# The last pack's gate and up weights in k-slices of four experts, and its last down piece as a half and two quarters

## The chip, the cores and the metric

The kernel runs on one core of one Trainium2 chip. The metric is the device time of one execution in microseconds (us); lower is better.

## The reference

The input is 256 tokens of width 1024, f32. A block of two token mixers (a gated short convolution and an S5 state model) is followed by a mixture of experts, and it is this second part that the change touches:

```
h2 = rms_norm(x, norm_ffn)
group, then top 2 of its 8 experts        # 4 groups x 8 = 32 experts
out = 0
for e in range(32):
    a = silu(h2 @ w_gate[e]) * (h2 @ w_up[e])      # 1024 -> 512
    out += combine[:, e] * (a @ w_down[e])         # 512 -> 1024
x = x + out
return rms_norm(x, norm_final)
```

All weights are f32. One expert's gate, up or down matrix is 2 MB, so the 96 of them are about 200 MB, which every execution reads once.

## The kernel before

**Packs.** The 32 experts are taken in 8 packs of 4. Each expert has 32 token slots, so a pack fills 128 slots. TensorE gathers the pack's tokens (L1340), multiplies them with gate into bank 4 and with up into bank 5, and the four experts of a pack run side by side, each with 32 columns of weights. ScalarE (ACT) takes silu of bank 4 (L675), VectorE (DVE) multiplies with bank 5 (L1045), TensorE transposes the product (L1358), ACT copies it to `actT` (L677), and TensorE multiplies it with the down weights: the left 512 columns of the result go to bank 6, the right 512 to bank 7. ACT copies the left half to `y_sb` (L680) and DVE the right half (L1049). Then TensorE adds both to the tokens with `wselT`, the transposed combine weights, in banks 0 to 3: bank 2b+h holds token block b (of 2) and column half h. These banks already hold the residual.

**Units.** Every weight transfer is a unit of 2 MB (16 KB in each of 128 partitions) in one of 11 slots, issued by SyncE (SP) in one queue in the order of `UNITS`. The transfer of unit v into a slot that is used again waits at L460 until `expert_units` says that unit v-11 is used. TensorE raises `expert_units` when a matrix product that read the units is done: for whole packs by four at a time (L1399, L1404).

**First and last pack.** Pack 0 has its own layout: eight `pair` units, each a quarter of k (256 of 1024 rows) of gate or of up for all four experts, in turn, and four `rows` units, each a quarter of the down rows (c) for all four experts. `first_pack` (L1407) multiplies each as it comes. Packs 1 to 6 use one unit for one expert's whole matrix (`whole_pack`, L1389), so a gate product starts when four units are there. The last pack (7) has four gate units and four up units of that kind (84 to 91), then three `rows` units (c = 0, 1, 2; 92 to 94), and c = 3 in two `half` units of 1 MB (95 and 96), left and right columns.

**The end.** `last_down` (L1455) multiplies the three rows units (L1443), then the left half unit (L1463), waits for ACT's copy, and adds block 0's left columns (L1451). Then come the product of the right half unit, the add of block 1's left columns, and, when DVE has copied the right half, the adds of blocks 0 and 1. Each of the four adds raises `moe_psum`. DVE then multiplies the left halves with the final norm's gain (`times_gain`, L1081); ACT squares each of the four banks for the norm (L702), and for the left ones it first waits for `times_gain` of the same bank. DVE (L734, L737) and GpSimd (POOL, L578) turn the sums into the scale, ACT and DVE scale the halves (L715, L1084), and SP stores two blocks (L501).

**keep_clock.** `keep_clock(to, n)` (L1107) puts n products of the identity with itself on TensorE, into a bank that is free. `first_pack` has nine of them after each of its first three rows units.

An f32 product shows as two records in the trace, so eight products of a rows unit (four experts, two halves) are 16 records.

Of the kernel before, what the change touches and what calls it, by code (L numbers as in the profile page):

```python
# [13 lines left out]
D = 1024  # L14
# [26 lines left out]
def expert_units_in_order():  # L41

    units = [(0, "pair", w) for w in range(8)] + [(0, "rows", c) for c in range(KF)]
    for pk in range(1, PACKS):
        units += [(pk, what, e) for what in ("gate", "up") for e in range(PACK)]  # L50
        if pk < PACKS - 1:
            units += [(pk, "down", e) for e in range(PACK)]
    last = PACKS - 1
    return units + [(last, "rows", c) for c in range(KF - 1)] + [(last, "half", h) for h in range(2)]
# [50 lines left out]
def block_kernel(nc, x_in, x_columns, columns, mix, s5_b, s5_c, norm_ffn, route_w, route_b, first, last_rows, last_halves,  # L105
# [10 lines left out]
    with ctx:  # L116
# [301 lines left out]
        def _(sp):  # L418
# [27 lines left out]
            def expert_source(pk, what, part):  # L446
                if what == "pair":
                    return first[part]
                if what == "rows":
                    return first[8 + part] if pk == 0 else last_rows[part]  # L450
                if what == "half":
                    return last_halves[part]
                view = {"gate": gate_v, "up": up_v, "down": down_v}[what]
                return view[:, pk * PACK + part, :]
# [127 lines left out]
        def _(act):  # L582
# [106 lines left out]
            def gate_used(pk):  # L689
                return expert_units, units_before(pk, ("gate",)) if pk else 7  # L690
# [28 lines left out]
        def _(dve):  # L719
# [315 lines left out]
            def expert_pack(o, done, number, rank_of, weight_of):  # L1035
# [12 lines left out]
                dve.wait_ge(down_psum[o], done * 2)  # L1048
                V.tensor_copy(y_sb[:, 512:D], bank[7][:]).then_inc(y_dve[o], 1)  # L1049

            def main_pack(pk):
                experts = slice(pk * PACK, (pk + 1) * PACK)
                if pk == 0:
                    dve.wait_ge(slots_moved, 1)
                    dve.wait_ge(rank_ready, 1)
                    dve.wait_ge(weight_ready, 1)
                expert_pack(0, pk + 1, slot_no[:], rank[:, :, experts], weight[:, :, experts])
# [45 lines left out]
        def _(pe):  # L1103
# [285 lines left out]
            def whole_pack(o, done, units, loaded_of, with_down=True):  # L1389
# [11 lines left out]
                if with_down:  # L1401
                    whole_down(o, done, loaded_of(2))
                    pe.wait_ge(down_psum[o], done * 2)
                    pe.sem_inc(units, PACK)  # L1404
                    combine(o, done)

            def first_pack():  # L1407

                tokens_in(0, 1)
                pe.wait_ge(xT_act[0], 1)  # L1410
                for w in range(8):
                    if w == 1:
                        rest_of_tokens(0, 1)
                    if w == 2:
                        pe.wait_ge(xT_act[0], 2)
                    if w == 4:
                        pe.wait_ge(xT_dve[0], 1)
                    wt = expert_view(expert_loaded(w), 1024)
# [7 lines left out]
                    else:  # L1426
                        ins.then_inc(up_psum[0], 1)
                        pe.wait_ge(up_psum[0], w - 5)
                        pe.sem_inc(expert_units, 1)
                turn_act(0, 1)  # L1430
# [19 lines left out]
            def combine_part(h, b):  # L1450
                ins = MM(bank[2 * b + h][:], wselT[:, b, :], y_sb[:, 512 * h:512 * h + 512],  # L1451
                         start=False, stop=True, skip_group_check=True)
                ins.then_inc(moe_psum, 1)

            def last_down():  # L1455

                first = units_before(PACKS - 1, ("gate", "up"))
                for c in range(KF - 1):
                    down_rows(0, c, expert_view(expert_loaded(first + c), D))
                for h in range(2):  # L1460
                    wt = expert_view(expert_loaded(first + KF - 1 + h), 512)
                    for e in range(PACK):
                        ins = MM(bank[6 + h][quarter(e), :], actT[:, KF - 1, quarter(e)], wt[:, e, :], start=False, stop=True)  # L1463
                    ins.then_inc(down_psum[0], 1)
                    if h == 0:
                        pe.wait_ge(y_act[0], PACKS)
                        combine_part(0, 0)
                combine_part(0, 1)
                pe.wait_ge(y_dve[0], PACKS)
                combine_part(1, 0)  # L1470
                combine_part(1, 1)
# [27 lines left out]
            whole_pack(0, PACKS, expert_units, main_loaded(PACKS - 1), with_down=False)  # L1499
            last_down()  # L1500
# [6 lines left out]
def laid_out(inputs):  # L1507
# [32 lines left out]
    def pack_of(name, pk, parts_of):  # L1540
# [5 lines left out]
    first = np.concatenate([pairs, pack_of("w_down", 0, KF).reshape(KF, P, UNIT)])  # L1546
    last = pack_of("w_down", PACKS - 1, KF)
    halves = last[KF - 1].reshape(P, PACK, 2, 512).transpose(2, 0, 1, 3)
# [3 lines left out]
            "last_rows": last[:KF - 1].reshape(KF - 1, P, UNIT), "last_halves": halves.reshape(2, P, UNIT // 2),  # L1552
# [19 lines left out]
```

## Time and profile before

| | |
|---|---|
| median of 3 runs | 717.51 us (717.11 to 720.56) |
| the profiled execution | 717.06 us |
| its span in the profile | 715.3 us |
| mean granted TensorE clock | 0.896 of 2.4 GHz |
| TensorE busy (matmuls) | 548.1 us, 77% |
| DVE, ACT, GpSimd busy | 206.6, 62.8, 39.8 us |
| data moved | 242.44 MB, mean 339 GB/s |

The profiled execution took 1.8 us more than its span: what lies around the span is not in the profile. A busy TensorE (PE) is one with a matmul under way; that says nothing of its speed, since its clock has two levels, 1.2 and 2.4 GHz (granted 0.50 and 1.00). PEld is the load of weights into TensorE, which overlaps matmuls. In "idle before", the releaser is what ended the wait, as the semaphores tell it.

### The profile page before, as it was taken

How to read it: one execution, taken by the hardware profiler on the slowest of the kernel's cores; microseconds unless marked ns; L12 is line 12 of the kernel's file. 1: busy time of each engine (PE TensorE's matmuls, PEld its weight loads, DVE VectorE, ACT ScalarE, POOL GpSimd, SP SyncE). 2: the span in 40 equal slices, each digit the busy share in tenths (PEclk: the TensorE clock that was granted, in tenths of full speed). 3: DMA queues.
4: the chain of work that ended last, by engine and by line, in shares of the span. 5: the costliest groups of instructions: out<-in, count | busy, mean ns of one | idle time of the engine just before them, and what ended most of it. 6: DMA issues, size and time to landing. Idle time of an engine off the chain costs nothing.

```text
span 715.3 us, 7547 instructions
## 1 busy us (share of the span) xinstructions
PE 548.1 (77%) x3241; PEld 329.0 (46%) x3241; DVE 206.6 (29%) x443; ACT 62.8 (9%) x126; POOL 39.8 (6%) x68
## 2 busy tenths in 40 slices
PE   8999999999999989898383484575558247457755
PEld 7888888888876646263141141122114014112411
DVE  4798897969421243000010010000001001000002
ACT  3010000002010032000000000000000000000102
POOL 5001111111100011000000000000000000000000
PEclk9999999999999999999796798779679669777889
DMA  9960804274097576999999999999999999999993
GB/s 340 426 275 9 344 1 148 87 297 174 1 394 311 206 306 242 414 434 425 427 433 427 426 433 426 429 428 431 429 424 432 427 429 429 430 429 424 432 424 153
DMA packets 19043, 242.44 MB, mean 339 GB/s; under 512 B 2368, under 2 KB 2496, under 8 KB 4544
## 3 DMA queue, kind: packets, MB, share of 16 engines
q1 hardware_dynamic: 18432, 239.83, 80.4%
q10 hardware_dynamic: 576, 2.10, 0.7%
q8 instruction: 28, 0.46, 0.3%
q14 instruction: 7, 0.06, 0.0%
HBM read 240.87 MB, written 1.05 MB: 338 GB/s over the span
## 4 chain that ended last, share of the span: by engine, by line
PE 52%; DMA 42%; DVE 2%; ACT 1%; issue 1%; POOL 0%; DVEq 0%; PEldq 0%; SPq 0%; ACTq 0%; POOLq 0%
PE bank L1121 27%; DMA ring<-in_w_down 13%; DMA ring<-in_w_gate 13%; PE bank L1373 8%; DMA ring<-in_w_up 8%; DMA s_region<-in_w_up 4%; DMA x_region<-in_w_up 4%; PE bank L1381 4%; PE bank L1255 4%; PE bank L1133 2%; PE bank L1422 2%; PE bank L1443 1%; PE bank L1225 1%; PE bank L1340 1%; PE bank L1235 1%
## 5 line engine op out<-in xcount | busy, mean ns | idle before, releaser
L1373 PE MATMUL bank<-ring,z_region 128*32 128x512 f32 x688 | 118.0, 674 | 63.9 <-DMA ring<-in_w_gate 15.2
L1121 PE MATMUL bank<-x_region,ring 128*128 128x256 f32 x640 | 141.0, 381 | 1.7 <-ACT ring L620 1.1
L1121 PEld LDWEIGHTS bank<-x_region,ring 128*128 128x128 f32 x640 | 120.8, 190 | 21.3 <-ACT ring L620 2.8
L1373 PEld LDWEIGHTS bank<-ring,z_region 128*32 128x32 f32 x688 | 33.6, 122 | 123.6 <-issue 123.6
L1381 PE MATMUL bank<-ring,m_region 128*32 128x512 f32 x240 | 54.9, 745 | 26.9 <-DMA ring<-in_w_down 16.1
L1045 DVE TENSOR_TENSOR z_region<-z_region,bank 128x512 f32<-128x512 f32 x8 | 8.2, 1027 | 209.4 <-PE bank L1373 197.3
L1373 PE MATMUL bank<-x_region,z_region 128*32 128x512 f32 x80 | 44.6, 722 | 10.7 <-DMA ring<-in_w_up 10.7
L1049 DVE COPY m_region<-bank 128x512 f32<-128x512 f32 x8 | 5.5, 692 | 139.3 <-PE bank L1381 111.3
L1381 PE MATMUL bank<-s_region,m_region 128*32 128x512 f32 x64 | 36.4, 734 | 8.6 <-DMA ring<-in_w_down 8.6
L1373 PE MATMUL bank<-rot_region,z_region 128*32 128x512 f32 x64 | 37.4, 750 | 7.0 <-DMA ring<-in_w_up 7.0
L1340 PE MATMUL bank<-conv_region,h_region 128*128 128x128 f32 x256 | 33.9, 288 | 4.5 <-issue 3.9
L1340 PEld LDWEIGHTS bank<-conv_region,h_region 128*128 128x128 f32 x256 | 32.7, 204 | 9.2 <-issue 9.2
L1373 PE MATMUL bank<-s_region,z_region 128*32 128x512 f32 x64 | 35.4, 716 | 0.8 <-issue 0.8
L1381 PEld LDWEIGHTS bank<-ring,m_region 128*32 128x32 f32 x240 | 13.3, 133 | 44.6 <-issue 44.6
L1381 PE MATMUL bank<-rot_region,m_region 128*32 128x512 f32 x48 | 26.9, 725 | 8.3 <-DMA ring<-in_w_down 8.3
L1121 PE MATMUL bank<-y_region,ring 128*128 128x256 f32 x128 | 28.9, 380 | 1.4 <-ACT y_region L625 1.4
L1255 PE MATMUL bank<-ring,m_region 128*128 128x512 f32 x64 | 28.7, 593 | 0.3 <-PE bank L1121 0.3
L1121 PE MATMUL bank<-z_region,ring 128*128 128x256 f32 x128 | 28.1, 380 | 0.0
L1121 PEld LDWEIGHTS bank<-y_region,ring 128*128 128x128 f32 x128 | 24.2, 190 | 7.6 <-issue 2.9
L1366 PE MATMUL bank<-m_region,conv_region 128*128 128x512 f32 x56 | 25.7, 601 | 1.2 <-PE bank L1381 1.1
L1121 PEld LDWEIGHTS bank<-z_region,ring 128*128 128x128 f32 x128 | 24.2, 190 | 3.7 <-DVE m_region L937 0.4
L578 POOL TENSOR_TENSOR stat<-stat,halfneg 128x1 f32<-128x1 f32 x2 | 1.1, 558 | 431.7 <-DVE stat L737 431.7
(244 smaller groups left out, 549.6 us busy)
## 6 DMA issues: line engine op xcount, KB each, us to landing
ring<-in_w_gate SPq DMA_DIRECT2D x26, 2048.0 KB, 34.5
ring<-in_w_up SPq DMA_DIRECT2D x17, 2048.0 KB, 34.0
ring<-in_mix SPq DMA_DIRECT2D x16, 2048.0 KB, 10.6
ring<-in_w_down SPq DMA_DIRECT2D x15, 2048.0 KB, 35.1
ring<-in_first SPq DMA_DIRECT2D x8, 2048.0 KB, 12.7
s_region<-in_w_down SPq DMA_DIRECT2D x4, 2048.0 KB, 36.2
x_region<-in_w_up SPq DMA_DIRECT2D x4, 2048.0 KB, 36.9
rot_region<-in_w_up SPq DMA_DIRECT2D x4, 2048.0 KB, 36.0
```

What stands on the lines that cost most here:

```text
L1045: V.tensor_tensor(act_sb.rearrange("p c q -> p q c"), silu.rearrange("p (q c) -> p q c", c=KF), bank[5][:].rearrange("p (q c) -> p q c", c ...
L1121: ins = MM(dst, w[:, k, n * P:(n + 1) * P], rhs[:, k, :], start=k == 0, stop=k == kn - 1)
L1133: ins = MM(bank[U_BANKS[n]][:, 0:T], w8(U_U)[:, k, n * P:(n + 1) * P], h_raw[:, k, :], start=k == 0, stop=k == KD - 1)
L1225: ins = MM(bank[4 + q][:, i * T:(i + 1) * T], BT[row_tile(q), b, i, :], uT[row_tile(q), b, :], start=True, stop=True)
L1235: ins = MM(bank[Y_BANK][row_tile(q), 0:T], CT[:, i, b, row_tile(q)], state(4 * b + q)[:, i, :], start=i == 0, stop=i == 1)
L1255: ins = MM(bank[4 + 2 * b + h][:], mixed[:, k, b * P:(b + 1) * P], w4(U_WO[k // 4])[:, k % 4, 512 * h:512 * h + 512], start=k == 0, stop=k ...
L1340: ins = MM(bank[GATHER_BANKS[part]][:, at:at + P], h2[:, b, k, :], sel[:, b].rearrange("p e s -> p (e s)"), start=b == 0, stop=b == TB - 1)
L1366: MM(bank[2 * b + h][:], wselT[:, b, :], y_sb[:, 512 * h:512 * h + 512], start=False, stop=True, skip_group_check=True)
L1373: ins = MM(bank[to][quarter(e), :], xT[:, k, quarter(e)], of_expert[e][:, FF * k:FF * k + FF], start=k == 0, stop=k == KD - 1)
L1381: ins = MM(bank[6 + h][quarter(e), :], actT[:, c, quarter(e)], of_expert[e][:, D * c + 512 * h:D * c + 512 * h + 512], start=c == 0, stop= ...
L1422: ins = MM(bank[4 + w % 2][quarter(e), :], xT[:, k, quarter(e)], wt[:, e, FF * kk:FF * kk + FF], start=k == 0, stop=k == KD - 1)
L1443: ins = MM(bank[6 + h][quarter(e), :], actT[:, c, quarter(e)], wt[:, e, 512 * h:512 * h + 512], start=c == 0, stop=c == KF - 1)
```

## The change

The order of the units and their data:

- Pack 7's gate and up come as eight `pair` units (84 to 91), laid out as those of pack 0. The number of units and bytes up to there is the same.
- The three rows units stay. The last part of down (c = 3) comes as one `half` unit (1 MB, left 512 columns; unit 95) and two `quarter` units (0.5 MB each, 256 columns; 96 and 97).

On TensorE, `last_pack` takes the place of `whole_pack` without down and of `last_down`. The loop over pairs of `first_pack` is now `paired_gate_up`, which both use. In the last pack it puts `keep_clock(7, 12)` after the sixth and the seventh pair (w = 5 and 6). Each rows unit is multiplied in three column groups instead of two: 512 columns to bank 6, 256 to bank 7, 256 to bank 5. After the rows come three parts in turn. Each part is: wait for the unit, multiply, wait for the copy to `y_sb`, and add to both token blocks.

On DVE the right half's copy is two copies of 256 columns, and `times_gain` comes after ACT's square of the same bank instead of ahead of it. On ACT the left squares wait only for `moe_psum` 1 and 2, the right ones for 5 and 6, and the last scaling (L715) waits for `fg_ready`.

```
-    return units + [(last, "rows", c) for c in range(KF - 1)] + [(last, "half", h) for h in range(2)]
+    units += [(last, "pair", w) for w in range(8)] + [(last, "rows", c) for c in range(KF - 1)]
+    return units + [(last, "half", 0), (last, "quarter", 0), (last, "quarter", 1)]
...
             for h in range(2):
-                act.wait_ge(moe_psum, 2 * h + 1)
-                if h == 0:
-                    act.wait_ge(fg_ready, 1)
-                square(0, h)
-                act.wait_ge(moe_psum, 2 * h + 2)
-                if h == 0:
-                    act.wait_ge(fg_ready, 2)
-                square(1, h)
-            for b in range(TB):
+                for b in range(TB):
+                    act.wait_ge(moe_psum, (1, 5)[h] + b)
+                    square(b, h)
+            for b in range(TB):
+                act.wait_ge(fg_ready, b + 1)
                 act.wait_ge(rstd, 3 + b)
...
-                dve.wait_ge(down_psum[o], done * 2)
-                V.tensor_copy(y_sb[:, 512:D], bank[7][:]).then_inc(y_dve[o], 1)
+                for i in range(parts):
+                    dve.wait_ge(down_psum[o], done * 2 + i)
+                    n = 512 // parts
+                    V.tensor_copy(y_sb[:, 512 + n * i:512 + n * i + n], bank[(7, 5)[i]][:, 0:n]).then_inc(y_dve[o], 1)
...
             for b in range(TB):
-                dve.wait_ge(moe_psum, b + 1)
-                times_gain(b, 0)
-            for b in range(TB):
                 dve.wait_ge(sumsq, 2 + 1 + b)
                 left_mean(b)
+                times_gain(b, 0)
...
+                    if done > 1 and w in (5, 6):
+                        keep_clock(7, 12)
...
+            def last_pack():
+                tokens_in(0, PACKS)
+                rest_of_tokens(0, PACKS)
+                pe.wait_ge(xT_act[0], PACKS * 2)
+                pe.wait_ge(xT_dve[0], PACKS)
+                first = units_before(PACKS - 1)
+                paired_gate_up(PACKS, first)
+                turn_act(0, PACKS)
+                columns = ((6, 0, 512), (7, 512, 256), (5, 768, 256))
+                def product(c, part, wt):
+                    to, _, n = columns[part]
+                    for e in range(PACK):
+                        ins = MM(bank[to][quarter(e), 0:n], actT[:, c, quarter(e)], wt[:, e, :], start=c == 0, stop=c == KF - 1)
+                    return ins
+                def add_to_tokens(part):
+                    _, at, n = columns[part]
+                    for b in range(TB):
+                        MM(bank[2 * b + at // 512][:, at % 512:at % 512 + n], wselT[:, b, :], y_sb[:, at:at + n],
+                           start=False, stop=True, skip_group_check=True).then_inc(moe_psum, 1)
                 for c in range(KF - 1):
+                    wt = expert_view(expert_loaded(first + 8 + c), D)
+                    for part, (_, at, n) in enumerate(columns):
+                        ins = product(c, part, wt[:, :, at:at + n])
+                    ins.then_inc(expert_units, 1)
+                for part, (_, at, n) in enumerate(columns):
+                    wt = expert_view(expert_loaded(first + 8 + KF - 1 + part), n)
+                    product(KF - 1, part, wt).then_inc(down_psum[0], 1)
+                    if part == 0:
                         pe.wait_ge(y_act[0], PACKS)
+                    else:
+                        pe.wait_ge(y_dve[0], PACKS - 1 + part)
+                    add_to_tokens(part)
```

## Rows read from the trace of the kernel before

**Rows 1.** The page's part 2: GB/s in 40 equal slices of the span.

```profile
GB/s 340 426 275 9 344 1 148 87 297 174 1 394 311 206 306 242 414 434 425 427 433 427 426 433 426 429 428 431 429 424 432 427 429 429 430 429 424 432 424 153
```

**Rows 2.** The timeline of SP's queue: start us, us from first to last issue.

```profile
637.21 19.04 SPq L468 DMA_DIRECT2D ring<-in_w_up  x2
656.29 1.38 SPq L468 DMA_DIRECT2D ring<-in_last_rows  x3
678.04 0.80 SPq L468 DMA_DIRECT2D ring<-in_last_halves  x2
```

**Rows 3.** DMA issues of short stretches: KB each, median us from issue to landing.

```profile
ring<-in_w_up SPq DMA_DIRECT2D x1, 2048.0 KB, 42.7
...
ring<-in_last_rows SPq DMA_DIRECT2D x1, 2048.0 KB, 33.4
...
ring<-in_last_halves SPq DMA_DIRECT2D x1, 1024.0 KB, 23.9
ring<-in_last_halves SPq DMA_DIRECT2D x2, 1024.0 KB, 24.9
```

**Rows 4.** The chain of work that ended last: start us, us, what.

```profile
655.92 28.88 DMA ring<-in_w_up
...
684.94 9.18 PE bank L1373 x64
...
694.21 1.03 DVE z_region L1045
...
696.63 5.36 PE bank L1443 x48
701.99 1.10 PE bank L1463 x8
...
703.11 0.61 ACT m_region L680
```

**Rows 5.** TensorE's timeline in the last pack, and one row of pack 0.

```profile
307.35 2.27 PE L1110 MATMUL bank<-ident 128*128 128x128 f32 x18
...
670.83 0.63 PE L1373 MATMUL bank<-ring,z_region 128*32 128x512 f32 x3 [0.80 <-issue]
...
703.76 1.13 PE L1451 MATMUL bank<-m_region,conv_region 128*128 128x512 f32 x2 [0.72 <-ACT m_region L680]
704.82 1.07 PE L1463 MATMUL bank<-ring,m_region 128*32 128x512 f32 x8
705.81 2.87 PE L1451 MATMUL bank<-m_region,conv_region 128*128 128x512 f32 x6
```

**Rows 6.** The timelines of DVE and ACT in the last 10 us.

```profile
705.95 0.69 DVE L1049 COPY m_region<-bank 128x512 f32<-128x512 f32 x1 [10.72 <-PE bank L1463]
...
707.33 0.60 ACT L702 ACTIVATE z_region<-bank 128x512 f32<-128x512 f32 x1 [3.62 <-DVE h_region L1081]
...
709.09 0.60 ACT L702 ACTIVATE z_region<-bank 128x512 f32<-128x512 f32 x1
...
709.30 0.21 DVE L737 TENSOR_SCALAR stat<-stat 128x1 f32<-128x1 f32 x1 [0.50 <-ACT z_region L702]
```

**Rows 7.** Groups of instructions: xcount | busy us, mean ns of one | idle before.

```profile
L1121 PE MATMUL bank<-z_region,ring 128*128 128x256 f32 x128 | 28.1, 380 | 0.0
...
L971 DVE COPY x_region<-bank 128x256 f32<-128x256 f32 x4 | 1.4, 418 | 0.8 <-PE bank L1289 0.8
```

**Rows 8.** Stretches: length, busy us of PE, PEld, DVE, ACT, POOL; PEclk, DMA share, GB/s.

```profile
677.90:682.30 4.40, 0.00 (x0) 0.00 (x0) 0.00 (x0) 0.60 (x1) 0.00 (x0) 1.00 0.98 421
684.94:689.17 4.23, 4.23 (x20) 1.09 (x24) 0.00 (x0) 0.00 (x0) 0.00 (x0) 0.50 1.01 426
297.30:299.80 2.50, 0.67 (x6) 0.43 (x6) 1.03 (x1) 0.60 (x1) 0.00 (x0) 1.00 1.07 459
299.79:303.17 3.38, 3.38 (x16) 0.59 (x16) 0.00 (x0) 0.00 (x0) 0.00 (x0) 0.54 1.03 441
694.10:696.60 2.50, 0.66 (x4) 0.42 (x4) 1.02 (x1) 0.60 (x1) 0.00 (x0) 1.00 1.02 429
```

More of the change, by code:

```diff
@@ L48, in expert_units_in_order @@
     units = [(0, "pair", w) for w in range(8)] + [(0, "rows", c) for c in range(KF)]
[L49 to L52, printed above, removed]
+    for pk in range(1, PACKS - 1):
+        units += [(pk, what, e) for what in ("gate", "up", "down") for e in range(PACK)]
     last = PACKS - 1
-    return units + [(last, "rows", c) for c in range(KF - 1)] + [(last, "half", h) for h in range(2)]
+    units += [(last, "pair", w) for w in range(8)] + [(last, "rows", c) for c in range(KF - 1)]
+    return units + [(last, "half", 0), (last, "quarter", 0), (last, "quarter", 1)]
 UNITS = expert_units_in_order()
@@ L102, in mixer_schedule, with block_kernel @@
     return order + [("ypre", YB - 1), ("gelu", YB - 1)]
-def block_kernel(nc, x_in, x_columns, columns, mix, s5_b, s5_c, norm_ffn, route_w, route_b, first, last_rows, last_halves,
+def block_kernel(nc, x_in, x_columns, columns, mix, s5_b, s5_c, norm_ffn, route_w, route_b, first, last_pairs, last_rows, last_half, last_quarters,
                  w_gate, w_up, w_down, norm_final, out):
@@ L447, in expert_source @@
                 if what == "pair":
-                    return first[part]
+                    return first[part] if pk == 0 else last_pairs[part]
                 if what == "rows":
@@ L451, in expert_source @@
                 if what == "half":
-                    return last_halves[part]
+                    return last_half
+                if what == "quarter":
+                    return last_quarters[part]
                 view = {"gate": gate_v, "up": up_v, "down": down_v}[what]
@@ L689, in gate_used @@
             def gate_used(pk):
-                return expert_units, units_before(pk, ("gate",)) if pk else 7
+                return expert_units, units_before(pk) + 7 if pk in (0, PACKS - 1) else units_before(pk, ("gate",))
             for pk in range(PACKS - 1):
@@ L1032, in _, with expert_pack @@
             V.tensor_copy(most[:], cnt_f[:]).then_inc(most_ready, 1)
-            def expert_pack(o, done, number, rank_of, weight_of):
+            def expert_pack(o, done, number, rank_of, weight_of, parts=1):
                 shape = [P, TB, PACK, SLOTS]
@@ L1056, in main_pack @@
                     dve.wait_ge(weight_ready, 1)
-                expert_pack(0, pk + 1, slot_no[:], rank[:, :, experts], weight[:, :, experts])
+                expert_pack(0, pk + 1, slot_no[:], rank[:, :, experts], weight[:, :, experts],
+                            parts=2 if pk == PACKS - 1 else 1)
             def over_experts():
@@ L1387, in rest_of_tokens, with whole_pack @@
                 pe.wait_ge(wselT_ready[o], done)
-            def whole_pack(o, done, units, loaded_of, with_down=True):
+            def whole_pack(o, done, units, loaded_of):
                 tokens_in(o, done)
@@ L1400, in whole_pack, with paired_gate_up @@
                 turn_act(o, done)
[L1401 to L1410, printed above, removed]
+                whole_down(o, done, loaded_of(2))
+                pe.wait_ge(down_psum[o], done * 2)
+                pe.sem_inc(units, PACK)
+                combine(o, done)
+            def paired_gate_up(done, first):
                 for w in range(8):
-                    if w == 1:
+                    if done == 1 and w == 1:
                         rest_of_tokens(0, 1)
-                    if w == 2:
+                    if done == 1 and w == 2:
                         pe.wait_ge(xT_act[0], 2)
-                    if w == 4:
+                    if done == 1 and w == 4:
                         pe.wait_ge(xT_dve[0], 1)
-                    wt = expert_view(expert_loaded(w), 1024)
+                    wt = expert_view(expert_loaded(first + w), 1024)
                     for kk in range(2):
@@ L1498, in _ @@
                 pe.sem_inc(over_done, 1)
-            whole_pack(0, PACKS, expert_units, main_loaded(PACKS - 1), with_down=False)
-            last_down()
+            last_pack()
 def in_tiles(w, tiles, columns):
@@ L1546, in laid_out @@
     first = np.concatenate([pairs, pack_of("w_down", 0, KF).reshape(KF, P, UNIT)])
+    last_pairs = np.stack([pack_of("w_gate", PACKS - 1, 4), pack_of("w_up", PACKS - 1, 4)], axis=1).reshape(8, P, UNIT)
     last = pack_of("w_down", PACKS - 1, KF)
-    halves = last[KF - 1].reshape(P, PACK, 2, 512).transpose(2, 0, 1, 3)
+    final = last[KF - 1].reshape(P, PACK, D)
+    quarters = final[:, :, 512:].reshape(P, PACK, 2, 256).transpose(2, 0, 1, 3).reshape(2, P, UNIT // 4)
     x_columns = one["x"].reshape(T, U_PIECES, 2, P).transpose(1, 3, 2, 0).reshape(U_PIECES, P, 2 * T)
@@ L1551, in laid_out @@
             "norm_ffn": inputs["norm_ffn"], "route_w": route_w, "route_b": route_b, "first": first,
-            "last_rows": last[:KF - 1].reshape(KF - 1, P, UNIT), "last_halves": halves.reshape(2, P, UNIT // 2),
+            "last_pairs": last_pairs, "last_rows": last[:KF - 1].reshape(KF - 1, P, UNIT), "last_half": final[:, :, :512].reshape(P, UNIT // 2), "last_quarters": quarters,
             "w_gate": inputs["w_gate"], "w_up": inputs["w_up"], "w_down": inputs["w_down"],
```

24 lines of the change are left out of this document (5 added, 19 removed).

## The prediction

> **What bounds the kernel now.** Read first the GB/s by slices: from the 17th slice to the last but one, 411 us, the core moves 414 to 434 GB/s without a hole [rows 1]. That is the weight stream, and what computes beside it costs nothing as long as the stream never waits for a slot and the work is done when the last piece lands. Then SP's timeline: the three rows units are issued at 656.3 and the halves at 678.0 [rows 2]. By the issue rows the last up unit lands at 655.9 + 28.9 = 684.8, the first rows unit at 656.3 + 33.4 = 689.7, the left half at 678.0 + 23.9 = 701.9; the right half, 1 MB behind it at about 427 GB/s, at 704.4, which the mean of 24.9 for both confirms [rows 3]. So 2 MB take 4.9 us, and the other rows units land at 694.6 and 699.5. The halves were issued 24 us ahead of landing: the stream does not wait for slots here, it is bytes that set these times.
>
> The chain that ended last shows where the stream hands over: last up unit to 684.8, up product 684.94 to 694.12, DVE, transposes and ACT to 696.63, the rows product to 701.99, left half 701.99 to 703.09, ACT's copy, and from 703.76 the adds [rows 4]. The rows product is 48 records in 5.36 us with about 0.2 us of drain at the end, so 1.72 us a unit. It ends within 0.1 us of the left half's landing: before the change, TensorE is just in time. The end behind it is 715.3 - 701.9 = 13.4 us, and it is TensorE's, not the stream's: the right half has landed at 704.4, and its product starts at 704.82, behind the first add [rows 5].
>
> **Pairs in place of whole matrices.** Same bytes, same shapes, same order of slots. Loads: unit 95 now waits for pair 0's product and not for all four gate units, so it is issued some 5 us sooner; with the stream full that is worth 0, and it would be worth something only if the queue ran dry, which needs more than 20 us of delay. TensorE starts at 670.83 as before [rows 5]. Six pairs of 16 records at 1.72 us: 681.15; all six have landed, the sixth at 675.0 (two units ahead of the last at 684.8). Each `keep_clock(12)` is 24 records; 18 records took 2.27 us in pack 0 [rows 5], so 3.0 us. Hence 684.2; seventh pair (landed 637.21 + 42.7 = 679.9 [rows 2, 3]) to 685.9, 0.2 us drain, keep_clock to 689.1, eighth pair (landed 684.8) to 690.8, drain to 691.0. Up is done 3.1 us sooner than at 694.12, not 7 us, since the keep_clocks stand between. The same 2.5 us of DVE, transposes and ACT [rows 4] put the rows at 693.5. Rows 0 (landed) to 695.2, rows 1 (landed 694.6) to 696.95, then a wait of 2.5 us for rows 2 at 699.5, to 701.2 and drained 701.4. The left half lands at 701.9. The 3.1 us are hidden: they become a wait for rows 2 and 0.5 us ahead of the left half. **Gain 0** in this execution; in one where the clock rises later than the 4.23 us after 684.94 seen here [rows 8], the old order would be late by half of that delay, so a gain of up to 0.5 us is possible. I take 0.2 for the median, which at 717.51 stands 0.45 above the profiled 717.06.
>
> **The clock.** The new 2.5 us wait sits behind a stretch (691.0 to 693.5) with only transposes. What do the rows say of such gaps? After a 2.5 us stretch with 0.67 us of transposes, pack 0's first rows unit ran at 0.54 and took 3.38 us in place of 1.9 [rows 8]. A gap of the same make at 694.10 was followed by full speed: the rows product behind it ran at 1.72 us a unit [rows 4, 8]. In the pause of 677.9 to 682.3 the grant still read 1.00, but the product at 684.94 ran its first 4.23 us at 0.50, the lower level of 1.2 GHz [rows 8]. So it may go either way, and pack 0 has fillers between rows units where the last pack has none. If it falls, rows 2 takes 3.44 us from 699.5 and ends at 702.94 or, if the grant comes back within it, some tenths earlier; the left half's product is then 0.5 to 1.8 us late, typically 0.9. Bounds: 0 and +2.5 us (rows 2, the left product and part of the adds slow). The two rows nearest in shape differ, so I take the middle, **+0.5**. The Trainium skill ("TensorE: Matmul & The Clock Gate", the section on HAM oscillation in real kernels) warns against just this: product bursts shorter than the DMA wait between them, each of which then starts at the low clock. By that rule the term would be 0.9; the row of pack 0 agrees with it, the one at 694.10 does not.
>
> **The last piece in three parts.** The parts run strictly in turn on TensorE. Start from 703.76, when ACT has copied the left half, as before (701.9 + product 1.06 + copy). Before, one add (0.86), the right product, the other left add under DVE's copy, then two right adds. Now:
> - Two left adds at once, 2 x 0.86 (two 0.43 records each): 705.48. Going from an add to a tiled product costs 0.2 us: 703.76 + 0.86 = 704.62, and the product came at 704.82 though its data had landed at 704.4 [rows 5]. So 705.68.
> - First quarter's product: half the columns, so 0.43 if records of 256 columns start every 0.22 us, as 128 of them in 28.1 us do [rows 7]; at most 0.86 if fewer columns save nothing. Drain 0.2: 706.31. DVE's copy of 256 columns is 0.42 [rows 7], not 0.69 [rows 6], plus 0.12 of handing over: 706.85. Two adds of 256 columns, 0.86: 707.71, and 0.2 again: 707.91.
> - Second quarter (long landed): product 0.43, drain 0.2, copy 0.54: 709.08. Adds 0.43 each with drain 0.2: done at 709.71 and 710.14.
>
> Before, the four adds were done at 705.81 + 2.87 = 708.68 [rows 5]. So TensorE ends 1.46 us later. The halved last piece helps only a kernel that waits for the last piece; this one comes to it 3.5 us late (707.91 against 704.4), and it now has two waits on DVE in series, in neither of which another product stands ready.
>
> **Squares and gains.** Before, the first square waited for `times_gain` until 707.33, four squares at 0.57 us brought the last to 709.09, 0.4 us behind the last add [rows 6]. Now both left squares are done by 707 and the right ones follow their adds: 709.76 and 710.33. The last starts 710.33 - 709.09 = 1.24 us later than before: the sooner squares give back 0.2 of the 1.46. DVE now has the second copy to 709.02, then mean, gain, mean, gain, 1.6 us: 710.6, and only then row_mean, which was at 709.30 [rows 6]: **+1.3 us**. Behind it pow, scaling and store are the same; the wait of L715 for `fg_ready` is met. If 256 columns saved nothing in the products: +0.9 more; if the switches cost nothing: -0.4.
>
> **Sum.** 717.06 (span 715.3 and 1.8 around it) + 1.3 + 0.5 = 718.9; with 0.2 of the median's distance kept, **719.1 us**, 1.6 above the median of the runs shown.
>
> **Rivals.**
> 1. Nothing to be seen, within 0.5 us of 717.5. For it: the median of before may hold 0.5 us of late rows product that goes away, the clock may stay up, and switches may overlap. Against: the two serial copies. It needs the 1.3 to be under 0.7. Time 717.6.
> 2. The low clock lasts. From 699.5 to the end of the left adds TensorE has 1.72 + 0.86 + 1.72 us of work at full speed; all of it at 1.2 GHz puts the end of the left adds at 709.0, not 705.5: +3.5 us, 717.06 + 1.3 + 3.5 = 721.9. For it: no filler after the rows. Against: work at 684.94 got the full clock in 4.23 us [rows 8], which from 699.5 is 703.7. It decides if the grant has not come back by 704.
> 3. Faster: the last landing sets the end, as a smaller last piece would want. Counted from 704.4: product 0.63, copy 0.54, adds 1.06, so the last add at 706.7, the last square at 706.8 instead of 709.09: 717.06 - 2.3 = 714.8. For it: the left half is issued 5 us sooner. It decides if the left half lands 3.5 us sooner, at 698.4. Against: rows 2, ahead of it in the queue, lands at 699.5, and the stream has no gap to give [rows 1].
>
> The Trainium skill ("DMA: Bandwidth & Descriptors", "Anatomy of one DMA") gives about 2.0 us fixed for each transfer. Were that paid in series for the extra piece, the second quarter would land near 706.4, still ahead of 707.91; the landing rows here, 4.9 us for 2 MB, show no such term in a full queue.
>
> **Chances.** Forecast (718.1 to 720.4) 0.64; rival 1, 0.18; rival 2, 0.09; rival 3, 0.05; something else 0.04. Range: from inside rival 1 to short of rival 2, 717.0 to 721.0. What a measurement can tell from no change is about 0.5%, 3.6 us: 713.9 to 721.1. Faster than that 0.03, within 0.88, slower 0.09.
>
> **What would show it.** In the profile after: GB/s unchanged until the last slice; up product done near 691; a TensorE wait of 2 to 3 us for the third rows unit; the left half's product at 702 to 703.5; the second quarter's product 3 us or more after its landing; the adds ending near 710 to 711; DVE's row mean about 1.3 us later. Wrong if the left half lands at another time than 702, if the quarter products take as long as halves, or if the grant is at 0.50 beyond 704.

## The result and the profile after

| | before | after |
|---|---|---|
| median | 717.67 us (716.27 to 720.56, 20 runs) | 720.38 us (718.99 to 722.29, 20 runs) |
| ratio after/before, 95% interval | | 1.0036 (1.0024 to 1.0047) |
| profiled execution, its span | 717.06, 715.3 us | 722.02, 720.3 us |
| granted clock | 0.896 | 0.900 |

The changed kernel is slower by 0.36%, some 2.6 us (1.7 to 3.4). The profiled execution is 1.6 us above its kernel's median, so its 5.0 us of longer span are not all the change's: the unit that lands at 331.5 us in the profile before lands at 332.8 here, 1.3 us later, ahead of everything that the change touches.

The GB/s by slices after, as [rows 1] before:

```profile
GB/s 339 424 271 18 333 1 178 56 331 137 15 421 312 157 360 200 414 427 429 428 432 426 432 425 427 431 429 427 430 428 427 432 427 428 430 427 429 426 412 89
```

The weight stream is as full as before. The lines below are the DMA issues of the end, with the time from issue to landing. The issues are at 656.53 (first rows unit), 657.48 (third), 672.77 (half), 674.49 and 676.2 (quarters), as [rows 2, 3]:

```profile
ring<-in_last_rows SPq DMA_DIRECT2D x1, 2048.0 KB, 34.6
...
ring<-in_last_rows SPq DMA_DIRECT2D x1, 2048.0 KB, 44.7
...
ring<-in_last_half SPq DMA_DIRECT2D x1, 1024.0 KB, 31.8
...
ring<-in_last_quarters SPq DMA_DIRECT2D x1, 512.0 KB, 31.4
```

So the first rows unit lands at 691.2, 1.5 us later than before; 1.3 of them are those of the early unit. The second follows at 696.05 (4.9 us). The third lands at 702.16, **6.1 us** behind it, the half at 704.6. The quarters land at 705.86 and 707.09. The earlier issue of the half by 5 us brought nothing: it waited 31.8 us in the queue instead of 23.9.

TensorE's timeline of the last pack after, as [rows 5]:

```profile
681.23 2.94 PE L1108 MATMUL bank<-ident 128*128 128x128 f32 x24
684.11 1.92 PE L1417 MATMUL bank<-ring,z_region 128*32 128x512 f32 x16
686.21 2.92 PE L1108 MATMUL bank<-ident 128*128 128x128 f32 x24 [0.18 <-PE bank L1417]
689.06 1.92 PE L1417 MATMUL bank<-ring,z_region 128*32 128x512 f32 x16
692.20 0.66 PE L1356 MATMUL bank<-ident,z_region 128*128 128x128 f32 x4 [1.22 <-DVE z_region L1042]
693.54 1.93 PE L1467 MATMUL bank<-ring,m_region 128*32 128x512 f32 x24 [0.69 <-ACT m_region L678]
696.09 1.93 PE L1467 MATMUL bank<-ring,m_region 128*32 128x512 f32 x24 [0.62 <-DMA ring<-in_last_rows]
702.21 4.39 PE L1467 MATMUL bank<-ring,m_region 128*32 128x512 f32 x32 [4.19 <-DMA ring<-in_last_rows]
707.32 1.98 PE L1473 MATMUL bank<-m_region,conv_region 128*128 128x512 f32 x4 [0.73 <-ACT m_region L681]
709.23 0.64 PE L1467 MATMUL bank<-ring,m_region 128*32 128x256 f32 x8
710.42 1.13 PE L1473 MATMUL bank<-m_region,conv_region 128*128 128x256 f32 x4 [0.55 <-DVE m_region L1048]
711.48 0.64 PE L1467 MATMUL bank<-ring,m_region 128*32 128x256 f32 x8
712.67 1.13 PE L1473 MATMUL bank<-m_region,conv_region 128*128 128x256 f32 x4 [0.55 <-DVE m_region L1048]
```

The up product ends at 691.0, then the rows units wait for data, the third for 4.19 us. From there on TensorE sets the end. It multiplies a quarter, waits for DVE's copy and adds, twice over: the two 0.55 us waits for L1048 are the serial parts. The clock of three stretches, columns as in [rows 8]:

```profile
698.00:702.10 4.10, 0.02 (x3) 0.00 (x0) 0.00 (x0) 0.00 (x0) 0.00 (x0) 1.00 0.90 369
702.21:705.40 3.19, 3.19 (x24) 1.18 (x28) 0.00 (x0) 0.00 (x0) 0.00 (x0) 0.50 0.41 170
705.50:713.80 8.30, 6.48 (x40) 2.47 (x32) 2.04 (x6) 2.37 (x6) 0.00 (x0) 1.00 0.01 3
```

TensorE sat idle from 698.0 to 702.1, and the third unit ran at 1.2 GHz (0.50) for 3.3 us. The clock was back when the left half's product began at 705.56, 0.9 us later than its data allowed. The last squares, as [rows 6]:

```profile
709.34 0.60 ACT L703 ACTIVATE z_region<-bank 128x512 f32<-128x512 f32 x1 [0.17 <-PE bank L1473]
...
713.40 0.60 ACT L703 ACTIVATE z_region<-bank 128x512 f32<-128x512 f32 x1 [3.37 <-PE bank L1473]
...
713.99 0.59 ACT L703 ACTIVATE z_region<-bank 128x512 f32<-128x512 f32 x1
```

ACT waits 3.37 us for the right adds. The third of the squares also sets when DVE's row mean starts:

```profile
714.20 0.21 DVE L734 TENSOR_SCALAR stat<-stat 128x1 f32<-128x1 f32 x1 [0.27 <-ACT z_region L703]
```

Two differences of landmarks compare all runs below: **landing to end**, from the left half's landing to the end of the span (before 715.33 - 701.94 = 13.39 us, after 720.29 - 704.60 = 15.69 us), and **third behind second**, between the landings of the second and third rows units (4.90 before, 6.11 after).

### The profile page after: what moved, and what is told of

Its sections match the earlier page's. It is cut to its first block, busy times and chain, and to the rows that moved or that the text cites. A ratio compares the mean times of both kernels' runs of the same rounds, so it can differ in the third digit from the quotient of the medians.

```text
span 720.3 us, 7714 instructions
## 1 busy us (share of the span) xinstructions
PE 549.0 (76%) x3325; PEld 333.1 (46%) x3325; DVE 206.5 (29%) x444; ACT 63.0 (9%) x126; POOL 39.8 (6%) x68
## 4 chain that ended last, share of the span: by engine, by line
DMA 48%; PE 47%; DVE 2%; SPq 1%; issue 1%; ACT 1%; POOL 0%; DVEq 0%; PEldq 0%; POOLq 0%
PE bank L1119 26%; DMA ring<-in_w_down 13%; DMA ring<-in_w_gate 13%; PE bank L1371 7%; DMA ring<-in_last_rows 6%; DMA s_region<-in_w_up 4%; DMA x_region<-in_w_up 4%; DMA ring<-in_w_up 4%; PE bank L1379 4%; PE bank L1253 4%; DMA ring<-in_mix 3%; PE bank L1417 2%; PE bank L1467 1%; PE bank L1297 1%; PE bank L1223 1%
## 5 line engine op out<-in xcount | busy, mean ns | idle before, releaser
L1371 PE MATMUL bank<-ring,z_region 128*32 128x512 f32 x608 | 99.8, 672 | 63.4 <-DMA ring<-in_w_gate 15.7
L1371 PEld LDWEIGHTS bank<-ring,z_region 128*32 128x32 f32 x608 | 28.5, 122 | 118.8 <-issue 118.8
L1048 DVE COPY m_region<-bank 128x512 f32<-128x512 f32 (+1 forms) x9 | 5.7, 632 | 147.1 <-PE bank L1379 111.9
L1371 PE MATMUL bank<-x_region,z_region 128*32 128x512 f32 x64 | 35.2, 714 | 12.4 <-DMA ring<-in_w_up 12.4
L1338 PEld LDWEIGHTS bank<-conv_region,h_region 128*128 128x128 f32 x256 | 31.8, 199 | 9.7 <-issue 9.7
L1371 PE MATMUL bank<-rot_region,z_region 128*32 128x512 f32 x48 | 26.9, 725 | 0.0
L1379 PE MATMUL bank<-x_region,m_region 128*32 128x512 f32 x32 | 18.6, 746 | 9.0 <-DMA ring<-in_w_down 9.0
```

The lines of the kernel that those rows point to most:

```text
L1048: V.tensor_copy(y_sb[:, 512 + n * i:512 + n * i + n], bank[(7, 5)[i]][:, 0:n]).then_inc(y_dve[o], 1)
L1338: ins = MM(bank[GATHER_BANKS[part]][:, at:at + P], h2[:, b, k, :], sel[:, b].rearrange("p e s -> p (e s)"), start=b == 0, stop=b == TB - 1)
L1371: ins = MM(bank[to][quarter(e), :], xT[:, k, quarter(e)], of_expert[e][:, FF * k:FF * k + FF], start=k == 0, stop=k == KD - 1)
L1379: ins = MM(bank[6 + h][quarter(e), :], actT[:, c, quarter(e)], of_expert[e][:, D * c + 512 * h:D * c + 512 * h + 512], start=c == 0, stop= ...
```

## The experiments

Differences are to the kernel before, from the ratio (times 717.7 us), with 95% intervals. "Grant" is the clock's level over the third rows unit and the left half's product, in the profiled execution. Each experiment has one profile. Theories A, B and C are the serial end, the clock and the instruction fetch; the expectations state them.

| kernel | difference, us | landing to end | third behind second | grant |
|---|---|---|---|---|
| before | 0 | 13.39 | 4.90 | 1.00 |
| changed | +2.6 (1.7 to 3.4) | 15.69 | 6.11 | mostly 0.50 |
| 1 pairs only | +1.8 (0.8 to 2.8) | 14.38 | 5.40 | mostly 0.50 |
| 2 end only | +1.1 (0.1 to 2.2) | 14.80 | 4.93 | 1.00 |
| 3 interleaved | +1.4 (0.4 to 2.4) | 12.85 | 5.72 | 1.00 |
| 4 fillers 8 | +2.7 (1.6 to 3.9) | 14.79 | 5.23 | 1.00 |
| 5 fill behind rows | +1.5 (0.7 to 2.4) | 14.79 | 5.56 | 1.00 |
| 6 end only, interleaved | -1.3 (-2.1 to -0.5) | 12.83 | 4.89 | 1.00 |
| 7 old squares | +3.6 (2.4 to 4.8) | 15.83 | 6.28 | 1.00 |
| 8 no fillers | +1.4 (0.4 to 2.2) | 14.80 | 4.89 | 1.00 |
| 9 fillers 4 | +3.3 (2.4 to 4.3) | 16.77 | 5.79 | 0.50 |
| 10 squares only | -0.6 (-1.3 to 0.0) | 12.82 | 4.89 | 1.00 |
| 11 no fillers, interleaved | +0.3 (-0.6 to 1.1) | 13.75 | 4.89 | mostly 0.50 |
| 12 interleaved, fill | -0.1 (-1.1 to 0.8) | 12.84 | 5.93 | 1.00 |

**1. Pairs only.** The end is that of the kernel before.

```
-    return units + [(last, "half", 0), (last, "quarter", 0), (last, "quarter", 1)]
+    return units + [(last, "half", h) for h in range(2)]
```

> The last pack's gate and up as pairs with their keep_clocks; the last down piece as two halves, the adds and the squares in the order of the kernel before. Theory A (the loss is the three parts in turn behind the left half): the adds follow as before the change, so from the left half's landing to the end 13.4 us when the clock is full, and against the kernel before 0 to +0.5 us. Theory B (the pairs bring a wait for the third rows unit and the low clock behind it): +0.5 to +1.5 us, with the grant at 0.50 when that unit starts. Theory C (a 16 KB instruction fetch for TensorE falls among the rows units and holds up the third by 1.2 us; here TensorE issues 32 instead of 48 instructions a rows unit, so the fetch is asked for only when the third unit has landed): the third rows unit lands 4.9 us after the second. If C is wrong and the delay comes from the pairs or their layout, it lands 6.1 us after it.

Measured +1.8 us: more than A gave, and above the upper end of B's 0.5 to 1.5 us, though its interval reaches into it. In its profile the third rows unit is 0.5 us late, the stretch behind it was granted 0.57, and landing to end is 1.0 us over before's 13.39. The pairs with their fillers lose by themselves. C's forecast of the place of the fetch failed here: the instruction packet started 1.5 us behind the second rows unit, 3.9 us ahead of the third.

**2. End only.** Gate and up as before the change, by `whole_gate_up` and per-expert units; the changed end.

> The last pack's gate and up as whole matrices, as before; the end as in the change (half, two quarters, parts in turn, sooner squares). Theory A: +1.3 us against the kernel before, with the last square 8.4 us after the left half's landing (7.1 before). Theory B: rows units one behind the other at full clock, so nothing of the clock's cost: the whole loss is A's. Rival (the loss comes with the pairs): 0 to +0.3 us.

Measured +1.1 us (theory A gave +1.3), and 14.80 us from landing to end, 1.41 over before, at full clock. In this profile the last quarter landed at 706.49, 0.9 us later than its place behind the first, without effect: its product started at 709.06.

**3. Interleaved.**

```
-                for part, (_, at, n) in enumerate(columns):
-                    wt = expert_view(expert_loaded(first + 8 + KF - 1 + part), n)
-                    product(KF - 1, part, wt).then_inc(down_psum[0], 1)
...
-                    add_to_tokens(part)
+                last_product(0)
+                last_product(1)
+                pe.wait_ge(y_act[0], PACKS)
+                add_to_tokens(0)
+                last_product(2)
+                pe.wait_ge(y_dve[0], PACKS)
+                add_to_tokens(1)
+                pe.wait_ge(y_dve[0], PACKS + 1)
+                add_to_tokens(2)
```

> The changed kernel with TensorE's order at the end alone altered: left product, first quarter's product, both left adds, second quarter's product, adds of the first quarter, adds of the second. Theory A: both waits for VectorE's copies go, the last add ends 1.8 to 2.0 us sooner, so +0.6 to +0.9 us against the kernel before in place of +2.6. Rival (the landing of the quarters or the squares set the end): still +2 or more.

Landing to end fell to 12.85 us, 1.94 below 14.79. TensorE's timeline of this kernel shows it: no wait for DVE is left.

```profile
703.19 1.06 PE L1467 MATMUL bank<-ring,m_region 128*32 128x512 f32 x8 [0.52 <-DMA ring<-in_last_half]
704.44 0.64 PE L1467 MATMUL bank<-ring,m_region 128*32 128x256 f32 x8 [0.19 <-DMA ring<-in_last_quarters]
705.01 1.98 PE L1473 MATMUL bank<-m_region,conv_region 128*128 128x512 f32 x4
706.92 0.64 PE L1467 MATMUL bank<-ring,m_region 128*32 128x256 f32 x8
707.49 1.99 PE L1473 MATMUL bank<-m_region,conv_region 128*128 128x256 f32 x8
```

The time fell from +2.6 to +1.4, less than the +0.6 to +0.9 that were expected, with an interval that holds them. What stays is the pairs' and their fillers': the sixth experiment has the same end without them.

**4. Fillers 8.** `keep_clock(7, 8)` in place of `keep_clock(7, 12)`.

> The changed kernel with keep_clock(7, 8) in place of keep_clock(7, 12), 32 TensorE instructions fewer ahead of the rows units. Theory C (the instruction fetch goes by the count of TensorE's instructions and holds up the transfer that it meets): it is asked for only when the third rows unit has started, so this unit lands 4.9 us after the second, not 6.1, and the time is 1.0 to 1.2 us below the changed kernel's: +1.4 to +1.6 us against the kernel before. Rival (the 6.1 us are chance or come from the small transfers behind): lands 6.1 us after it or varies from run to run, and the time stays at +2.6.

A miss: +2.7 us, and the fetch still fell between the second and third unit. Its profile holds another answer: the clock was full at the third unit, and the same end takes 14.79 us. So 0.9 of the changed profile's 15.69 are the clock's. No filler stood behind the second rows unit here, so the clock can stay up without one.

**5. Fill behind rows.**

```
                     ins.then_inc(expert_units, 1)
+                    if c == 1:
+                        keep_clock(4, 12)
```

> The changed kernel with keep_clock(4, 12), 3.0 us of fillers, behind the second rows unit. Theory B (the wait for the third rows unit lets the clock fall, which then costs some tenths to 1 us in the third unit and the left half's product): the grant is 1.00 when the third unit starts, from the left half's landing to the end 14.8 us (15.7 in the changed kernel's profile), and over many executions about 0.5 us is saved: +2.1 us against the kernel before. Rival (the clock seldom falls, or it comes back in time): no difference to the changed kernel's +2.6.

Full clock, 14.79 us, +1.5 us against the changed kernel's +2.6. The intervals overlap; the sign is theory B's, and the size, 1.1 us, is twice what it gave. The full clock of the one profile proves little by itself: 3, 4, 7 and 8 have it without this filler. The third experiment and the twelfth are a second pair with and without it, +1.4 and -0.1.

**6. End only, interleaved.** The second kernel with the third's order.

> Gate and up as whole matrices, as before the change; half and two quarters, sooner squares, and TensorE's products and adds interleaved as in the third experiment. Both parts that lose are gone. Theories A and B: left half's landing to the end 12.8 us in place of 13.4, and -0.2 to -0.7 us against the kernel before. Rival (the quarters cost something by themselves, as transfers or since an instruction fetch meets the last of them): 0 to +1 us, with the last quarter's landing more than 1.3 us behind the first's.

-1.3 us (-2.1 to -0.5), more than the 0.2 to 0.7 us that were expected, better than both kernels of the case, and 12.83 us from landing to end.

**7. Old squares.**

```
                     act.wait_ge(moe_psum, (1, 5)[h] + b)
+                    if h == 0:
+                        act.wait_ge(fg_ready, b + 1)
                     square(b, h)
```

> The changed kernel with the order of squares and gains of the kernel before (the left squares wait for times_gain, which VectorE does behind its second copy). By the timelines times_gain of block 0 then starts with the end of the second copy, all four squares follow it at 0.57 us each, and the last one starts 1.1 us later than in the changed kernel: left half's landing to the end 15.8 to 16.0 us at full clock, +3.5 to +3.9 us against the kernel before. Rival (the sooner squares give nothing): +2.6.

15.83 against 14.79 at full clock: 1.04 us for the order of the squares; +3.6 us. The edit to squares and gains is a gain inside the change.

**8. No fillers.** Both `keep_clock(7, 12)` removed.

> The changed kernel without the two keep_clock(7, 12) among the pairs. TensorE is then some 3 us sooner through with up and waits 3 us or more for each rows unit; no grant of 1.00 should hold through the rows. Theory B: the clock is at 0.50 when the third unit starts in nearly every execution, +0.2 to +1.0 us against the changed kernel, so +2.8 to +3.6 against the kernel before. Rival (the fillers among the pairs only hold TensorE up): +2.6 or less.

+1.4 us, against the expectation: better than the changed kernel. Its profile shows two things. The granted clock fell twice, so that the eighth pair and the first rows unit took 3.44 and 3.20 us in place of 1.92, but it was back at 1.00 for the second and third:

```profile
684.41 3.44 PE L1417 MATMUL bank<-ring,z_region 128*32 128x512 f32 x16 [2.97 <-DMA ring<-in_last_pairs]
...
690.42 3.20 PE L1465 MATMUL bank<-ring,m_region 128*32 128x512 f32 x24 [0.69 <-ACT m_region L678]
694.20 1.97 PE L1465 MATMUL bank<-ring,m_region 128*32 128x512 f32 x24 [0.58 <-DMA ring<-in_last_rows]
699.09 1.93 PE L1465 MATMUL bank<-ring,m_region 128*32 128x512 f32 x24 [2.92 <-DMA ring<-in_last_rows]
```

And the third rows unit was on time: the instruction packet came 3.4 us behind its landing. One profile does not say how often the clock is as kind.

**9. Fillers 4.** `keep_clock(7, 4)`.

> The changed kernel with keep_clock(7, 4) in place of keep_clock(7, 12): 64 TensorE instructions fewer ahead of the rows units. In the traces so far TensorE's instruction fetch came 20 to 29 instructions ahead of the third rows unit's first with 12 or 8 fillers, and the unit landed 0.3 to 1.4 us late each time; with no fillers (96 instructions fewer) the fetch came behind that unit's landing, and it was on time. Theory C: with 64 fewer the fetch also comes behind the landing, the third unit lands 4.9 us after the second, and the time is some 0.8 us below the changed kernel's: +1.4 to +2.0 us against the kernel before. Rival (the fetch's place is chance and the fillers' own time is what counts): fetch between 696 and 699, third unit late, +2.6.

A miss for C's forecast of the place: with 64 instructions fewer the packet came at 698.8, still 2.2 us ahead of the third unit's landing, and the unit was 0.9 us late. It is the clearest case of theory B. TensorE was idle for 3.25 us ahead of the third unit, and the grant stayed at 0.50 through it and the left half:

```profile
697.80:700.90 3.10, 0.00 (x0) 0.00 (x0) 0.00 (x0) 0.00 (x0) 0.00 (x0) 0.50 0.93 378
700.97:706.30 5.33, 5.33 (x32) 1.38 (x32) 0.00 (x0) 0.00 (x0) 0.00 (x0) 0.50 0.27 112
```

The 32 records take 5.33 us (1.93 + 1.06 at full clock in the fourth experiment), and landing to end is 16.77, 2.0 us over 14.79: +3.3 us in the time.

**10. Squares only.** The kernel before with the order of squares and gains of the change.

> The kernel before with the order of squares and gains of the change alone: the left squares do not wait for times_gain. By the timeline of before, the last square starts when the last add is done, 708.74, and not at 709.09, and VectorE's gains do not hold up the row mean: -0.3 to -0.4 us. Rival (VectorE, which now does the gains behind its copy and the squares, becomes the last): 0 or +0.3 us.

12.82 us from landing to end, -0.6 us (-1.3 to 0.0), where -0.3 to -0.4 was expected. With two halves and two lines moved it has the same end as the sixth, with three pieces. Whether the quarters add anything to it cannot be told: the intervals overlap.

**11. No fillers, interleaved.**

> The changed kernel without the keep_clocks and with TensorE's end interleaved: pairs, quarters, sooner squares, no fillers. If the parts add up, this is the eighth experiment (+1.4 us) less the 1.95 us of the interleaving: -0.7 to -0.3 us against the kernel before, with the instruction fetch behind the third unit's landing, 12.8 us from the left half to the end at full clock. The sixth (whole matrices in place of pairs) gave -1.3 us. Theory B says that this one stays behind it, by the clock that the waits for the rows units let fall: 0 to +1 us above the sixth. Rival (pairs by themselves are worth something once fillers and order are out of the way): -1.5 us or less.

+0.3 us, against an expected -0.7 to -0.3. The grant fell in this profile (0.53 from the third unit's start), and landing to end is 13.75, 0.9 over 12.83. Against the sixth kernel, which differs in pairs or whole matrices alone, it is 1.6 us behind.

**12. Interleaved, fill.** The third and the fifth edit together.

> The changed kernel with both cures: TensorE's end interleaved, and keep_clock(4, 12) behind the second rows unit. If the costs add up, the serial end (1.95 us) and the clock are gone and what stays of the pairs is the late third rows unit: 12.8 us from the left half's landing to the end at full clock, the third unit 5.2 to 6.3 us behind the second with an instruction fetch between them, and 1.5 - 1.95 = -0.4 us against the kernel before, 0.5 to 1 us above the sixth experiment's -1.3. If the late unit costs nothing in the time, it equals the sixth: -1.3 us.

-0.1 us, with 12.84 us from landing to end at full clock: in this profile nothing of the serial end or the clock is left. It stays 1.2 us behind the sixth, and its third rows unit is 1.0 us late.

**The late third rows unit.** Beside the weights, the trace shows a queue for instructions, in transfers of one 16 KB packet, which take 1.0 to 1.4 us in the last pack. The packets between the landings of the second and third rows units, in the changed kernel (first) and in the eighth experiment (second):

```profile
## 3 DMA queue, kind: packets, MB, share of 16 engines
q1 hardware_dynamic: 338, 2.28, 91.6%
q8 instruction: 1, 0.02, 1.1%
```

```profile
## 3 DMA queue, kind: packets, MB, share of 16 engines
q1 hardware_dynamic: 275, 1.94, 96.9%
```

Eight kernels have such a packet there (changed, 1, 3, 4, 5, 7, 9, 12), and in all eight the third unit is late, by 0.3 to 1.4 us. Six have none (before, 2, 6, 8, 10, 11), and in all six it comes 4.89 to 4.93 us behind the second. That alone does not make the packet the cause, and packets fall into other units too. The landings of the shares show what it does. A weight unit arrives in 16 shares, each of which lands 4.9 us behind the same share of the unit ahead. In the changed kernel the share that was due at 700.60 landed at 702.16, the other 15 by 700.95. Between 676 and 700 us the 14 profiles have 22 such packets. With each of the 22 one share, and one only, came 1.5 to 1.7 us late; in the units of this stretch without a packet no share did. A unit is as late as its last share, so what it loses is the 1.5 us less the lead that the share had: in the changed kernel 1.2 us, but in the kernel before, where a packet started at 688.86, the share due at 693.00 landed at 694.52, ahead of the last one at 694.60, and nothing was lost. The tenth experiment has the same; in the second and sixth the second rows unit came 0.5 and 0.3 us late. What is lost stays lost: the left half follows the third unit by 2.3 to 2.5 us in all 14, so its landing moves with it.

When the packet comes goes by TensorE's instructions: the last one started when 6601 to 6678 of its records had begun, in all 14 profiles. The fillers are 96 of them. Without fillers (8, 11) it came 3.4 and 3.6 us behind the third unit's landing, and with whole matrices it came behind the left half's.

The Trainium skill ("Runtime: NRT & Kernel Launch", the section on instruction fetch mechanics) says that each engine's sequencer fetches its instructions in 16 KiB blocks by DMA, at a cost that is mostly hidden. The blocks agree; the cost is not hidden here, where a late share holds up the units for which the kernel waits.

## Why the prediction was right, and what was off

**Sign and size.** 719.1 us was forecast, in a range of 717.0 to 721.0, slower than before; 720.38 came out. The forecast loss was 1.6 us, the measured one 2.6 (1.7 to 3.4). The terms of the serial end and the clock hold as mechanisms; the pairs cost a third thing, for which the sum had nothing.

**The stream and the pairs' gain of 0: right.** GB/s unchanged, the half issued sooner with no effect, the up product done at 691.0, as the sum had it to the tenth. The 3.1 us became a wait for the third rows unit. The step that failed is a time in it: "a wait of 2.5 us for rows 2 at 699.5", counted as 4.9 us behind the second unit. It came 6.1 us behind, and TensorE waited 4.19 us. In the eight profiles with an instruction packet in between, this term is 0.3 to 1.4 us, and the prediction had no term for it. Its price in the time was not isolated: fewer fillers (4 and 9) left the packet within the transfer. What the sixth and twelfth kernels differ by, 1.2 us, is a rough size at most, since they differ in pairs and fillers too.

**The signs.** By the letter two signs of being wrong came. The left half landed at 704.6 and not at 702: 1.3 us of that were there at 333 us, 1.2 are the third unit's, and 0.2 came with the packet at 678.2. And the grant was at 0.50 until 705.5, beyond 704. Counted from the start of the third unit that is 3.3 us, where the 704 of the prediction stood for 4.5.

**The clock: right in kind, its size open.** I took +0.5 from bounds of 0 and 2.5 us. The eight profiles with pairs and no filler behind the second rows unit have 0 (3, 4, 7, 8), 0.9 (changed, 11), 1.0 (1) and 2.0 us (9), 0.6 in the mean. The length of the wait does not separate them: behind 3.25 us the seventh ran at full clock, behind 2.96 us the eleventh mostly at 0.50. The fill moved the time by 1.1 us (5 against the changed kernel) and by 1.5 us (12 against 3); in both pairs the intervals overlap, so 0.5 is not excluded. By the rule of the Trainium skill that was cited beside the term each of the eight would have paid; four did. That the sooner pairs bring the loss and not the gain is shown by the first experiment (+1.8 us with their fillers) and by 11 against 6 (1.6 us without). Of the 1.6, the profiles show 0.9 behind the left half's landing and 0.3 ahead of it; the rest is open.

**The serial end: right.** +1.3 us was the sum; four profiles at full clock have 14.79 or 14.80 us against 13.39, so +1.40. Its steps on TensorE hold one by one: adds of 256 columns at 0.43 us, product and drain 0.64, copy 0.42, product to second quarter's product 2.25 (709.23 to 711.48; the sum had 2.23). The interleaving, expected from the same rows at 1.8 to 2.0 us, gave 1.94. One step does not hold: the sum let DVE's mean and gains hold up the row mean, but DVE was through at 713.93 and waited 0.27 us for ACT's third square. That the number is right all the same is luck, since the sum had the squares 1.24 us later. The row mean stands 9.60 us behind the left half's landing against 7.36 before, 2.24 us, of which 0.9 are the clock's and 1.3 the end's.

**Squares and gains: right for this end.** "The sooner squares give back 0.2 of the 1.46". Against the old order in the new end they are worth 1.04 us, as expected for the seventh (1.1). In the end of before they are worth 0.57 us from landing to end where I had said 0.3 to 0.4.

**Late rows product of before.** I kept 0.2 us for an exposure of the old kernel in other executions. No run tells of it.

**Rivals.** Rival 1 needed the 1.3 us to be under 0.7, and they are not. Rival 2 asked for a low clock until the end of the left adds. The grant was back 3.3 us behind the third unit's start in the changed profile; experiment 9 came nearest, with 0.50 for 5.3 us. Rival 3 fell as it was argued: the left half did not land sooner.

**A fixed cost of each transfer.** The 2.0 us that the prediction quotes from the Trainium skill stand, in the section that it names, for transfers that GpSimd issues; these are SP's. The half and the quarters landed at 704.60, 705.86 and 707.09, so 0.5 MB took 1.24 to 1.25 us where 1 MB took 2.44: in the full queue no fixed term shows. No term of the sum hung on it.

## What to carry to other kernels

A smaller last piece can pay only if the engine behind the transfers is waiting for the last piece. Count from each landing to the moment at which that engine asks for it. Where copy and add of one piece alternate with the next piece's product, put that product ahead of the add: here 1.9 us of 14.8. Taking work as it arrives in a full stream turns one long product into bursts with waits between. What it wins in time can be paid back in clock: in four of eight profiles without a filler before the last wait, in neither of two with one. And fillers are instructions: they bring the next instruction packet forward, here into the transfer for which the kernel waits.

## What the runs showed of the hardware that was not expected

- With each of 22 instruction packets of 16 KB in the last pack, one of the 16 shares of the 2 MB units came 1.5 to 1.7 us late. The units lost 0 to 1.4 us by it, as the share had been ahead of the last one or not.
- The last such packet started when 6601 to 6678 of TensorE's records had begun, in 14 of 14 profiles. Removing 32 or 64 of its instructions left the packet within the third unit's transfer; removing 96 put it 3.4 us behind its landing.
- An idle stretch of 4.1 us ended with the grant still at 1.00 and the work behind it at 0.50, and the full clock came back 3.3 us into that work. In the ninth experiment, where the grant was at 0.50 before the third unit began, it stayed there for 5.3 us of work.
- Going from adds (128 weight columns) to a product (32) cost about 0.2 us each time: four records of 0.43 us took 1.91 until the product began (707.32 to 709.23), four of 0.22 took 1.06 (710.42 to 711.48).
